# Odd block: two query chunks inside the attention loop, and the band mask added by TensorE

## The reference, cut to what matters

```
q, k, v = split(h @ w_qkv)                       # 1024 | 256 | 256 columns, h is 256 x 1024
q, k = rope(q), rope(k)                          # own tokens; then k and v of the context are joined: 512 keys
s = (q @ k.T) * 64 ** -0.5                       # per head, 256 x 512
s = where(own key and |i - j| > 128, -inf, s)    # the band mask
p = exp(s - m) / (sum(exp(s - m)) + exp(sink - m))
out = (p @ v) @ w_out
```

## Time and profile before

| what | us |
|---|---|
| runs | 2183.05, 2184.37, 2187.43 (median 2184.37) |
| profiled execution | 2180.98 |
| its span | 2179.2 |
| TensorE busy | 2116.4 |
| VectorE busy | 1783.8 |
| ScalarE busy | 1176.2 |

### The profile page before, as it was taken

The page is one execution under the profiler, slowest core; times in us unless marked ns, Lnnn a source line. Parts: engine busy times, 40 slices in busy tenths (PEclk is TensorE's granted clock), DMA queues, the critical chain, the costliest instruction groups (busy, mean ns, idle before and its releaser), DMA issues.

```text
span 2179.2 us, 33377 instructions
## 1 busy us (share of the span) xinstructions
PE 2116.4 (97%) x13779; PEld 1852.4 (85%) x13788; DVE 1783.8 (82%) x2366; ACT 1176.2 (54%) x1756; POOL 109.9 (5%) x157
## 2 busy tenths in 40 slices
PE   7999999999999999999999999999999999999997
PEld 4888888888888889898888989988888888768886
DVE  4988787788878878877888877898998998788764
ACT  3554556455455535665554544547646744485742
POOL 1000000000000000000000000000000000000000
PEclk9999999999999999999999999999999999999999
DMA  9989666488868877655887747748878876405662
GB/s 333 292 286 315 222 228 202 147 265 275 309 195 286 280 267 239 221 192 173 275 280 276 241 155 231 238 131 293 279 265 295 298 260 238 136 18 159 211 212 78
DMA packets 331023, 506.51 MB, mean 232 GB/s; under 512 B 12391, under 2 KB 239942, under 8 KB 330871
## 3 DMA queue, kind: packets, MB, share of 16 engines
q1 hardware_dynamic: 288647, 342.01, 47.9%
q0 software_dynamic: 41616, 160.44, 21.3%
q10 hardware_dynamic: 608, 1.92, 0.3%
HBM read 503.29 MB, written 1.05 MB: 231 GB/s over the span
## 4 chain that ended last, share of the span: by engine, by line
PE 88%; DVE 8%; DMA 2%; ACT 1%; issue 1%; POOL 0%; DVEq 0%; POOLq 0%
PE banks L632 38%; PE banks L636 19%; PE banks L626 6%; PE banks L628 6%; PE banks L627 6%; DMA plain_xs<-in_ada_w_dram 1%; PE banks L838 1%; PE banks L900 1%; PE banks L733 1%; PE banks L735 1%; PE banks L734 1%; DVE wlo L2026 1%; DVE nraw L2304 1%; DMA stage<-in_ffn_wg_dram 1%; DVE arena L2051 1%
## 5 line engine op out<-in xcount | busy, mean ns | idle before, releaser
L2026 DVE TENSOR_TENSOR wlo<-stage,whi 128x1024 fp32r<-128x1024 f32 x644 | 758.2, 1219 | 128.5 <-ACT whi L1503 127.7
L1503 ACT CAST whi<-stage 128x1024 fp32r<-128x1024 f32 x644 | 644.0, 1052 | 334.9 <-PE banks L636 257.2
L632 PE MATMUL banks<-xs,whi 128*128 128x512 f32 x2176 | 686.2, 397 | 12.8 <-DVE xs L2308 9.6
L636 PEld LDWEIGHTS banks<-xs,wlo 128*128 128x128 f32 x2176 | 408.8, 188 | 96.6
L636 PE MATMUL banks<-xs,wlo 128*128 128x256 f32 x2176 | 427.6, 278 | 0.0
L626 PE MATMUL banks<-xs,whi 128*128 128x256 f32 x1216 | 351.2, 289 | 10.4 <-DVE xs L2308 5.7
L632 PEld LDWEIGHTS banks<-xs,whi 128*128 128x128 f32 x2176 | 331.1, 189 | 17.8 <-DVE xs L2308 7.6
L628 PE MATMUL banks<-xs,wlo 128*128 128x256 f32 x1216 | 343.9, 283 | 0.0
L627 PE MATMUL banks<-xs,whi 128*128 128x256 f32 x1216 | 343.9, 283 | 0.0
L632 PE MATMUL banks<-hidden_arena,whi 128*128 128x512 f32 x992 | 311.8, 395 | 0.0
L2051 DVE SCALAR_TENSOR_TENSOR arena<-modw,cact,arena 128x1024 f32<-128x1024 f32 x217 | 277.8, 1280 | 9.6 <-DMA modw<-in_w_mod_dram 6.3
(11 more groups left out here) (438 smaller groups left out, 2618.1 us busy)
## 6 DMA issues: line engine op xcount, KB each, us to landing
stage<-in_mlp_w_dram SPq DMA_DIRECT2D x96, 1024.0 KB, 5.3
modw<-in_w_mod_dram POOLq DMA_DIRECT2D x80, 1024.0 KB, 5.8
modw<-in_ada_w_dram POOLq DMA_DIRECT2D x66, 1024.0 KB, 5.5
stage<-in_ffn_wg_dram SPq DMA_DIRECT2D x44, 1024.0 KB, 5.4
stage<-in_ffn_wu_dram SPq DMA_DIRECT2D x44, 1024.0 KB, 7.3
stage<-in_ffn_wd_dram SPq DMA_DIRECT2D x44, 1024.0 KB, 7.5
stage<-in_ev_w_in_dram SPq DMA_DIRECT2D x24, 1024.0 KB, 5.8
stage<-in_w_in_dram SPq DMA_DIRECT2D x18, 1024.0 KB, 5.5
```

The source lines that it names most:

```text
L632: return mm(out, whi[:, s, w:w + P], pair.rearrange("p a t -> p (a t)"), start=first_mm, stop=False, skip_group_check=True)
L636: return mm(out[:, 0:T], wlo[:, s, w:w + P], pair[:, 0, :], start=False, stop=last_mm, skip_group_check=True)
L1503: nc.scalar.copy(halves(whi[:, s, :], n, h, True), halves(stage[:, s, :], n, h)).then_inc(hi_done, 1)
L2026: last = v.tensor_tensor(halves(wlo[:, s, :], n, h, True), halves(stage[:, s, :], n, h), halves(whi[:, s, :], n, h, True).bitcast(F32), AL ...
```

## The change

The mask goes from VectorE to TensorE. ScalarE makes three tiles `masks` (identity and the mask's two halves) as rounded floats, and `scores` adds identity times mask into the scores' banks with one more matmul for each of the two heads; VectorE's add is gone. Query chunks 4 and 5 leave the stretch before the loop: TensorE does their products in parts of 5, 6 and 5 block products in steps 0, 1, 2 and 5, 6, 7, between scores(s+2) and turn(s), in bank `Y[1]`, which `values` gives up (both pairs' results share `Y[0]` now, so that values of pair p wait for the output copy of p - 1). The duplicated keys move ahead of chunk 3. Rotation 3 moves between scores(1) and the loop, rotations 4 and 5 behind steps 3 and 8. Of the chunks n+6, n+7 and n+8 (output chunks 0, 1 and 2) the conversions on both engines go behind steps 1, 3 and 8 of the loop; ScalarE copies query chunks 4 and 5 out there too.

```diff
+        ROT_BANK = {0: 1, 2: 0, 3: 0, 4: 1, 5: 1}
+        QUERY_STEP = {4: 3, 8: 4, 12: 5}
+        QUERY_PARTS = {0: (4, 0, 5), 1: (4, 5, 11), 2: (4, 11, 16), 5: (5, 0, 5), 6: (5, 5, 11), 7: (5, 11, 16)}
...
+                def query_part(c, lo, hi):
+                    if lo == 0:
+                        pe.wait_ge(lo_done, START + n + c + 1)
+                        if c == 4:
+                            pe.wait_ge(drained.sem, drained.at(("od", 3)))
+                        else:
+                            pe.wait_ge(dve_out.sem, dve_out.at(("odrope", 4)))
+                    for i in range(lo, hi):
+                        f, k = i // 8, i % 8
+                        last = product(Y[:, 1, f * T:f * T + T], k * 256 + f * P, (xhi[:, k, :], xlo[:, k, :]), (n + c) % RING, k == 0, k == 7)
+                    if hi == 16:
+                        last.then_inc(chunk_used, 1)
...
-                        last = mm(R[:, 2 * (s % 2) + e, :], O["q"][64 * e:64 * e + 64, p, qt * P:(qt + 1) * P],
-                                  O["kdup"][64 * e:64 * e + 64, p // 2, :], start=True, stop=True)
+                        mm(R[:, 2 * (s % 2) + e, :], O["q"][64 * e:64 * e + 64, p, qt * P:(qt + 1) * P],
+                           O["kdup"][64 * e:64 * e + 64, p // 2, :], start=True, stop=False, skip_group_check=True)
+                    for e in range(2):
+                        last = mm(R[:, 2 * (s % 2) + e, far], masks[:, 0, :], masks[:, 1 + qt, :], start=False, stop=True, skip_group_check=True)
...
                 scores(0)
-                rot(5)
+                pe.wait_ge(drained.sem, drained.at(("od", 2)))
                 scores(1)
+                rot(3)
                 for s in range(16):
-                    if s == 2:
-                        pe.wait_ge(dve_out.sem, dve_out.at(("odrope", 3)))
+                    if s + 2 in QUERY_STEP:
+                        pe.wait_ge(dve_out.sem, dve_out.at(("odrope", QUERY_STEP[s + 2])))
                     if s + 2 < 16:
                         scores(s + 2)
+                    if s in QUERY_PARTS:
+                        query_part(*QUERY_PARTS[s])
                     turn(s)
                     if s >= 1:
                         values(s - 1)
+                    if s == 3:
+                        rot(4)
+                    if s == 8:
+                        rot(5)
...
+                        nc.scalar.copy(masks[:, 0, :], ident)
+                        nc.scalar.copy(masks[:, 1, :], qk_table[:, 0, P:2 * P])
+                        done(nc.scalar.copy(masks[:, 2, :], qk_table[:, 1, 0:P]), "masks")
...
+                    if s == 1:
+                        conv(n + 6)
+                    if s == 3:
+                        take_chunk(4)
+                        conv(n + 7)
+                    if s == 8:
+                        take_chunk(5)
+                        conv(n + 8)
...
-                    link(v.tensor_tensor(scores[:, :, far], scores[:, :, far], window[:, qt, far].unsqueeze(1).to_broadcast([P, 2, P]), ALU.add))
                     link(v.tensor_reduce(stat[:, o:o + 2], scores, AX_X, ALU.max))
...
                 maxima(0)
-                rotate(4)
+                rotate(3)
                 for s in range(16):
                     if s + 1 < 16:
                         maxima(s + 1)
                     normalise(s)
-                    if s == 0:
+                    if s == 1:
+                        conv(n + 6)
+                    if s == 3:
+                        conv(n + 7)
+                    if s == 4:
+                        rotate(4)
+                    if s == 8:
+                        conv(n + 8)
+                    if s == 9:
                         rotate(5)
```

## The result

The changed kernel takes 2197.43 us (median, 2196.11 to 2199.59) against 2184.82 of the kernel before in the same comparison: ratio 1.0058, 95% interval 1.0040 to 1.0075, 12.6 us slower. The forecast was +14.8 us and 2199.2.

The account below looks back on a forecast made before the run. The prediction took TensorE, busy 97% of the span, as the bound; 10.6 us for waits and masks plus 4.2 for the clock made +14.8, so 2199.2 us from a median of 2184.37, range 2188.0 to 2206.0.

Parts of the forecast that it names:

- (a): Two query chunks moved from before the loop into six parts: 0 us by itself, first scores near 1877.3.
- (b): 32 mask matmuls on TensorE, 2 per step, at 0.13 us each: 4.2 us, ends 1.9 and 7.7.
- (c): VectorE loses 16 mask adds, 7.4 us, in the loop: worth only the 0.8 us of small waits.
- The layout: The whole order laid out by hand with trace prices: TensorE waits 16.55 us against 10.2 before.
- (d): Three conversions in the loop, VectorE's waiting for ScalarE's: TensorE waits 2.46, 3.66 and 3.66 us, taking back 9.8.
- The layout's sum: 6.35 us of added TensorE waits plus 4.2 for the masks: +10.6 us.
- (e): Half clock behind the new waits in the loop: 2 falls, 5.0 us, less 0.8 taken up: 4.2, ends 0 and 7.5.
- (f): DMA of weight loads and output chunks, and values waiting for output copy p-1 in place of p-2: nothing.
- Rival A: Not slower, as the conversions' waits in the loop are covered: -0.4 us, 2184.0 or down to 2181; chance 0.20.
- Rival C: Mask matmuls at the full float price of 0.24 and three clock falls: +20.1 us, 2204.5; chance 0.12.

Follow-up runs that it names:

- Masks alone: The kernel before with the mask added by two TensorE matmuls and no VectorE add, nothing moved: 2185.21 us against 2183.98, ratio 1.0006.
- query parts only: The changed kernel with the mask taken off TensorE and added by VectorE as before: 2201.20 us against 2183.98 of the kernel before, ratio 1.0074.
- the later conversions: The changed kernel with VectorE's three conversions one step later each, behind steps 2, 4 and 9: 2186.36 us against 2183.98 of the kernel before, ratio 1.0010.
- the last two kernels: The changed kernel with VectorE's mask and conversions moved (2183.64 us, 0.9994 against before); from there, query parts, rotations, copies and conversions placed anew (2180.37 us, 0.9985).

## Why the prediction was right, point by point

- **(a) The move.** First scores with no new wait: held (1880.02, less the 2.8 us that the whole execution ran late, is 1877.2, for 1877.3 forecast); behind rotation 0 TensorE has none before scores 2. A part's first product after the masks costs 0.17 instead of 0.12, some 0.3 us over six parts, which I hadn't counted.
- **(b) Masks.** 4.2 us forecast. Measured 0.27 a pair, 4.3 in all, or 0.24 by what a step grows, 3.9. Held. The Trainium skill's 81 ns ("TensorE: Matmul & The Clock Gate", Back-to-back issue gap) doesn't describe this form: 0.12 to 0.14 us measured, and the measurement decides. A rounded-float matmul of 128 columns is no cheaper than one of 256 (0.12) here.
- **(c) VectorE's relief** was called worth 0.8 us. Masks alone cost 0.8 instead of 4.3, so it was worth 3.5 in the order of before, and this term was too small. In the changed order it is worth about as much: VectorE's chain is on the path three times, and taking the masks off TensorE again brought an estimated 0.8 us, not 4.3 (the 2.6 us by which that execution is longer are its clock falls). The layout had this in it: it waits for VectorE's works as they are, and its total doesn't rest on the 0.8.
- **(d) The three conversions.** Waits of 2.46, 3.66 and 3.66 forecast, 2.30, 3.30 and 3.31 measured (2.45, 3.47 and 3.47 by starts), released by VectorE as said, VectorE idle 4.79, 5.75 and 6.33 before its conversions. The last chain took 8.90 and not 7.9, as an output copy that waited for values stood in it; in the same time TensorE waited 0.96 for the chunk copy, which the forecast had as rotation 5's 0.97. Shown by moving VectorE's alone (8.8 us back) and by taking one out.
- **The layout's sum.** +10.6 forecast; the kernel that keeps TensorE busy in the waits has no clock falls and shows 101.54 - 91.15 = 10.4. Its waits, by starts, are some 16.1, for 16.55 laid out.
- **(e) The clock** is the term that was mis-sized: 4.2 forecast, 2.0 measured in this execution. The number of falls was right, two, but at turns 2 and 9, not 4 and 9, and they took 3.2 us for 5.0 forecast, as the half clock was shorter. Of the 3.2 a wait at turn 10 took up 1.1 and one at rotation 4 took up 0.1. Other kernels had falls at turn 4 or at all three; the same wait of 3.3 us kept full clock once and lost it once. So this term is a spread for this kernel, from 0 to an estimated 6 us (the 6.6 of the three falls with query parts only, less what turn 10 takes up), and not a number.
- **(f)** Nothing of the transfers or of the values' wait for the output copy shows in any of the lists of waits.
- **Rival A** (the conversions' waits are covered) needs VectorE not idle before them; it was, so A is out. Its price of -0.4, for conversions that wait for nothing, was reached by no run with the masks on TensorE: the later conversions, which still waited up to 2.09, bring the change to +3.6 in the inner stretch, +2.1 without its fall. The layouts below zero have the mask on VectorE and are not rival A's kernel. **Rival C**'s mask price of 0.24 is out.

The level came out nearer than the change by luck: +14.8 was forecast on a median of 2184.37 and +12.6 measured on 2184.82, so that 2199.2 is 1.8 us off and the change 2.2.

## What to carry to other kernels

Before a step is moved into a loop of several engines, look for the instruction that waits on another engine's late work, and add up what is queued behind it: with 2.36 us of conversion in it, 7.6 to 8.9 us passed from one turn to the next, because it stood one step too early in VectorE's queue. With the consumer a step behind the producer, 8.8 of the 12.4 us came back. And a schedule by hand with durations from the trace, checked first against the kernel before (91.2 us), gave three new orders within 0.2 us where the clock stayed up (10.6 for 10.4, 89.3 for 89.32, 87.3 for 87.44); so it can choose the order as well as explain it. It was 0.6 off for the masks alone (+1.4 for +0.8), and it can't say where the clock falls.

## What the runs showed of the hardware

- The clock's fall is no function of the one wait before it. Behind a wait of 3.30 to 3.31 us TensorE kept full clock in one execution and ran at half in another; behind 2.30 it fell, and in the kernel with VectorE's conversions later it fell around a wait of 1.02 that followed one of 0.79. Behind 1.72 it fell in the kernel before, and behind 1.92 at the same place it stayed at 1.00 in the last two kernels. Each fall cost 1.5 to 2.7 us of TensorE's work, and with matmuls of zeros in the waits none was seen. Part 1 of the Trainium skill's page "TensorE: Matmul & The Clock Gate" says that activity lifts the throttle, and that experiment agrees.
- A mask matmul of 128 columns behind two packed full float ones took 0.27 us a pair, and 0.23 for a second pair behind it. A step of 3.11 us became 3.35 with one pair.
